# Two decoder blocks on one core: sliding attention by pairs of heads, on two row halves and two column halves

## What is computed

```
q = proj[..., :OFF_K].reshape(b, l, ATTN_HEADS, HEAD_DIM)          # 16 heads of 64
k = proj[..., OFF_K:OFF_V].reshape(b, l, ATTN_KV_HEADS, HEAD_DIM)  # 4 heads of keys
v = proj[..., OFF_V:OFF_Z].reshape(b, l, ATTN_KV_HEADS, HEAD_DIM)
attn = windowed_gqa_sink(q, k, v, attn_sink[i])
...
s = jnp.einsum('bnqgrd,bnkgd->bngrqk', qb, kw) * (d ** -0.5) + bias[None]
m = jnp.maximum(jnp.max(s, axis=-1, keepdims=True), sink_f)
p = jnp.exp(s - m)
denom = jnp.sum(p, axis=-1, keepdims=True) + jnp.exp(sink_f - m)
o = jnp.einsum('bngrqk,bnkgd->bnqgrd', (p / denom), vw)
...
merged = (jax.nn.sigmoid(gate_a) * (attn @ w_attn_branch[i])
          + jax.nn.sigmoid(gate_b) * (ssd @ w_ssd_branch[i]))
```

## Time and profile before

| | |
|---|---|
| median of 3 runs | 2693.75 us (2691.79 to 2695.16) |
| profiled execution, its own time | 2694.09 us |
| its span | 2692.3 us |
| PE, busy share | 96% |
| DVE, ACT busy share | 55%, 43% |
| share of the chain that ended last: PE, DVE, ACT | 79%, 13%, 5% |
| matmul instructions | 12498 |
| granted PE clock, mean | 0.984 |
| DMA, mean | 84 GB/s |

### The profile page before, as it was taken

One profiled execution on the slowest core, in us unless ns is written; L12 is line 12 of the kernel. 1 busy time (PEld: TensorE's weight loads), 2 busy tenths in 40 slices (PEclk: granted clock), 3 DMA queues, 4 the chain that ended last, 5 costly groups with the idle time before them and its releaser, 6 DMA issues.

```text
span 2692.3 us, 31915 instructions
## 1 busy us (share of the span) xinstructions
PE 2591.8 (96%) x12498; PEld 2110.0 (78%) x12498; DVE 1471.4 (55%) x2343; ACT 1155.8 (43%) x2068; POOL 146.3 (5%) x144
## 2 busy tenths in 40 slices
PE   7999999999999999999999999999999999999998
PEld 5888778888676778888787888888777887788886
DVE  5554454433556555334369887886555355453343
ACT  4254443322356644223255666655244344442232
POOL 1110000000100010000001000100000010000000
PEclk9999999999999999999989999999999999999999
DMA  4212123653222122232223112123211243223331
GB/s 138 71 56 67 61 77 102 135 132 102 79 92 77 63 79 94 94 102 95 81 56 102 56 55 77 57 71 87 73 33 40 71 141 110 71 94 99 100 99 63
DMA packets 201110, 225.47 MB, mean 84 GB/s; under 512 B 25152, under 2 KB 133984, under 8 KB 200704
## 3 DMA queue, kind: packets, MB, share of 16 engines
q1 hardware_dynamic: 200960, 223.43, 27.6%
HBM read 213.96 MB, written 9.44 MB: 83 GB/s over the span
## 4 chain that ended last, share of the span: by engine, by line
PE 79%; DVE 13%; ACT 5%; issue 2%; POOL 0%; DMA 0%; DVEq 0%; POOLq 0%; SPq 0%; ACTq 0%
PE bank L1767 21%; PE bank L1769 20%; PE bank L1768 20%; DVE CV L2458 3%; PE bank L1773 2%; DVE wlo L2234 2%; PE bank L1774 2%; PE bank L1775 2%; PE bank L1785 2%; PE bank L1970 1%; PE bank L1802 1%; PE bank L1951 1%; DVE E L2507 1%; ACT whi L2017 1%; PE bank L1866 1%
## 5 line engine op out<-in xcount | busy, mean ns | idle before, releaser
L2234 DVE TENSOR_TENSOR wlo<-raw,whi 128x1024 fp32r<-128x1024 f32 (+1 forms) x389 | 489.4, 1263 | 738.0 <-ACT whi L2017 735.8
L2017 ACT ACTIVATE whi<-raw 128x1024 fp32r<-128x1024 f32 (+1 forms) x389 | 408.5, 1057 | 652.8 <-PE bank L1769 611.6
L1767 PE MATMUL bank<-XAh,whi 128*128 128x512 f32 x1536 | 618.8, 403 | 19.8 <-DVE XAl L2242 10.9
L1768 PE MATMUL bank<-XAl,whi 128*128 128x512 f32 x1536 | 604.6, 394 | 0.0
L1769 PE MATMUL bank<-XAh,wlo 128*128 128x512 f32 x1536 | 604.3, 393 | 0.0
L1767 PEld LDWEIGHTS bank<-XAh,whi 128*128 128x128 f32 x1536 | 292.1, 190 | 97.6 <-issue 32.2
L1769 PEld LDWEIGHTS bank<-XAh,wlo 128*128 128x128 f32 x1536 | 291.9, 190 | 63.2
L1768 PEld LDWEIGHTS bank<-XAl,whi 128*128 128x128 f32 x1536 | 292.4, 190 | 59.1 <-issue 0.7
L1767 PE MATMUL bank<-XBh,whi 128*128 128x512 f32 x816 | 324.2, 397 | 3.0 <-DVE XBl L2240 1.7
L1769 PE MATMUL bank<-XBh,wlo 128*128 128x512 f32 x816 | 318.0, 390 | 0.0
L1768 PE MATMUL bank<-XBl,whi 128*128 128x512 f32 x816 | 317.8, 389 | 0.0
(11 more groups left out here) (326 smaller groups left out, 3449.0 us busy)
## 6 DMA issues: line engine op xcount, KB each, us to landing
raw<-in_w_in SPq DMA_DIRECT2D x68, 512.0 KB, 3.7
raw<-in_up SPq DMA_DIRECT2D x64, 512.0 KB, 3.5
raw<-in_down SPq DMA_DIRECT2D x64, 512.0 KB, 3.7
raw<-in_a_w_in SPq DMA_DIRECT2D x32, 512.0 KB, 4.0
raw<-in_w_up SPq DMA_DIRECT2D x32, 512.0 KB, 3.6
raw<-in_w_down SPq DMA_DIRECT2D x32, 512.0 KB, 3.6
raw<-in_w_kv SPq DMA_DIRECT2D x16, 512.0 KB, 3.5
raw<-in_w_ssd_branch SPq DMA_DIRECT2D x16, 512.0 KB, 3.4
```

The lines of the kernel that those rows point to most:

```text
L1767: pe.matmul(out, wh[:, w, c], xh[:, x, 0:s.ntok], start=st, stop=False)
L1768: pe.matmul(out, wh[:, w, c], xl[:, x, 0:s.ntok], start=False, stop=False)
L2017: act.activation(s.hi, s.raw, ACT.Copy).then_inc(s.whi[0], 1)
L2234: dve.tensor_tensor(s.lo, s.raw, s.hi.bitcast(F32), ALU.subtract).then_inc(s.wlo[0], 1)
```

## The change

Heads are issued by pairs. Both heads of a pair use the same key head, but lie in the two row halves of one Q tile, in the weights' own order. So the keys are needed in both halves: a second tile `KD` holds `KW` with its halves exchanged, written by two transfers on SP's queue (`swap_k`). A step of scores is now one query block of both heads, two matmuls on the two row halves, into two banks. A step of values does all ten products of both heads alternately, on the two column halves of one bank. `SW` and `AW` become one ring of six. `KD` takes 4 KB a partition, and `NRAW` goes from 4 to 3, which gives 4 KB back. The pipeline holds three pairs, in the order 0 to 7, and `scoring` lets a third pair start its scores only when one of two is past its norms.

```
-NRAW, NW = 4, 3
+NRAW, NW = 3, 3
...
+    KD = sb("KD", [P, 2, S], scope=both)
...
+    def keys_evac(j, i, b, m):
+        yield from keys_rows(j, i, b, m)
+        if j[1]:
+            qk["swapped"] = add("swap_k", dst=KD, src=KW, ready=qk["k", 1], land=sig("swapped", 32)).land
...
-        return two_tiles([(64 * x, 64) for i in (2 * n, 2 * n + 1) for x in heads_of[i]], rows_evac(Q_tile, "q", n, free), ring=ring, piece=piece, gate=lambda: free in w_free)
+        return two_tiles([(n * 256, 256)], rows_evac(Q_tile, "q", n, free), ring=ring, piece=piece, gate=lambda: free in w_free)
...
-        SW = Ring([Slot(sb(f"SW{i}", [P, 4, 384], scope=sc)) for i in range(3)])
-        AW = Ring([Slot(sb(f"AW{i}", [P, 4, 384], scope=sc)) for i in range(3)])
+        SW = Ring([Slot(sb(f"SW{i}", [P, 4, 384], scope=sc)) for i in range(6)])
...
+        def head_pair(hp):
+
+            kv = hp // 2
+            keys = [(KW, KD)[(kv + x) % 2] for x in range(2)]
...
+            while (started[p.pieces] and not p.hurry) or scoring["n"] == 1 or not SW.room(2) or not ring_all.room(3) or ("q", hp) not in qk:
                 yield WAIT
...
+            ss = [SW.take(), SW.take()]
+            for j in range(4):
...
+                s1 = add("wi_mm", Q=Q_tile(hp), kws=keys, kv=kv, j=j, banks=bs, q_ready=qk["q", hp], k_ready=qk["k", kv // 2], swapped=qk["swapped"], mm=[sig("wi.mm"), sig("wi.mm")])
+                s2 = add("wi_bias", ss=ss, j=j, banks=bs, slopes=slopes, mm=s1.mm, pads=sw_pads, biased=[sig("wi.bias"), sig("wi.bias")])
...
+                if j == 1:
+                    yield from p.spaced(1)
+            begun, exps, normed = p.pieces, [], []
+            for x in range(2):
+                exps.append(add("wi_exp", s=ss[x], c=stw[:, 2 * hp + x, :], hd=2 * hp + x, slope=slopes[x], biased=s2.biased[x], top=sig("wi.top"), exp=sig("wi.exp")).exp)
+                yield
+                yield from p.spaced(1)
+            for x in range(2):
+                normed.append(add("wi_norm", s=ss[x], c=stw[:, 2 * hp + x, :], exp=exps[x], normed=sig("wi.norm")).normed)
+                yield
+                yield from p.spaced(1)
+            scoring["n"] -= 1
...
-        p.run(products_w(), pipeline((head_w(2 * hp + hx) for hp in (0, 2, 1, 3, 4, 6, 5, 7) for hx in range(2)), 6), starts=[9, 0])
+        p.run(products_w(), pipeline((head_pair(hp) for hp in range(8)), 3), starts=[9, 0])
...
+            for x, b in enumerate(s.banks):
+                rs = slice(64 * x, 64 * x + 64)
+                pe.matmul(b.t[:, 0:w], s.Q[rs, s.j * P:(s.j + 1) * P], s.kws[x][rs, s.kv // 2, lo * P:lo * P + w], start=True, stop=True).then_inc(s.mm[x][0], 1)
...
+                    for x, aw in enumerate(s.aws):
+                        m = pe.matmul(s.bank.t[x * 64:x * 64 + 64, j * P:(j + 1) * P], s.V[:, ks, s.kv * 64:s.kv * 64 + 64], aw.t[:, ks, q0:q0 + P], start=ks == lo, stop=ks == hi)
...
+        elif k == "swap_k":
+            on.wait_ge(*s.ready)
+            for x in range(2):
+                sp.dma_start(s.dst[64 * x:64 * x + 64, :, :], s.src[64 - 64 * x:128 - 64 * x, :, :]).then_inc(s.land[0], 16)
```

More of the change, by code:

```diff
@@ L1497, in branch_gemm @@
             return gemm(XB, 8, "w_attn_branch_2", [(hf * 512, 512)], fm4(), evac, ring=ring_all, piece=1)
[L1499 to L1504, removed]
+        def head_pair(hp):
+            kv = hp // 2
+            keys = [(KW, KD)[(kv + x) % 2] for x in range(2)]
+            slopes = [float(np.float32(2.0 ** (-8.0 * (2 * hp + x + 1) / 16))) for x in range(2)]
+            while (started[p.pieces] and not p.hurry) or scoring["n"] == 1 or not SW.room(2) or not ring_all.room(3) or ("q", hp) not in qk:
                 yield WAIT
             started[p.pieces] += 1
-            s = SW.take()
-            for j0 in (0, 2):
+            scoring["n"] += 1
+            ss = [SW.take(), SW.take()]
+            for j in range(4):
                 while not ring_all.room(2):
@@ L1516, in head_w @@
                 yield
-            begun = p.pieces
-            s3 = add("wi_exp", s=s, c=stw[:, hd, :], hd=hd, slope=slope, biased=s2.biased[1], top=sig("wi.top"), exp=sig("wi.exp"))
-            yield
[L1520 to L1546, removed]
@@ new lines, in head_pair @@
+            for x in range(2):
[3 more added lines that the diff above has]
+            scoring["n"] -= 1
+            aws, done = [], []
+            for x in range(2):
+                while not SW.room(1):
+                    yield WAIT
+                aws.append(SW.take())
+                for k0 in (0, 2):
+                    while not ring_all.room(2):
+                        yield WAIT
+                    bs = [ring_all.take(), ring_all.take()]
+                    s5 = add("wi_tr", s=ss[x], k0=k0, banks=bs, normed=normed[x], tr=[sig("wi.tr"), sig("wi.tr")])
+                    s6 = add("wi_aw", aw=aws[x], k0=k0, banks=bs, tr=s5.tr, scope_free=end, aw_done=[sig("wi.aw"), sig("wi.aw")])
+                    for b, v in zip(bs, s6.aw_done):
+                        b.free(v)
+                    yield
+                ss[x].free(s5.tr[1])
+                done.append(s6.aw_done[1])
+                yield from p.spaced(1)
@@ L1552, in head_w @@
+            yield from p.spaced(1)
+            while not ring_all.room(1) or ("v", 1) not in qk:
+                yield WAIT
+            ob = ring_all.take()
+            s7 = add("wi_val", V=VW, kv=kv, aws=aws, aw_ready=done, bank=ob, v_ready=[qk["v", x] for x in range(2)], val=sig("wi.val"))
+            for aw in aws:
+                aw.free(s7.val)
+            yield
+            yield from split_apart(XB, hp, ob.t[:, :], s7.val)
+            ob.free(XB.ready[hp])
             yield
         XB.open()
-        p.run(products_w(), pipeline((head_w(2 * hp + hx) for hp in (0, 2, 1, 3, 4, 6, 5, 7) for hx in range(2)), 6), starts=[9, 0])
+        p.run(products_w(), pipeline((head_pair(hp) for hp in range(8)), 3), starts=[9, 0])
@@ L2536, in dve_program @@
             on.wait_ge(*s.pads)
[L2537 to L2542, removed]
+            lo, w, off = win_span(s.j)
+            for x, (t, b) in enumerate(zip(s.ss, s.banks)):
+                on.room(t)
+                on.wait_ge(*s.mm[x])
+                dve.scalar_tensor_tensor(out=t.t[:, s.j, off:off + w], in0=b.t[:, 0:w], scalar=0.125 / s.slopes[x], in1=K.Rt[:, off:off + w], op0=ALU.mult, op1=ALU.add).then_inc(s.biased[x][0], 1)
         elif k == "wi_exp":
```

25 lines of the change are left out of this document (9 added, 16 removed).

## The result

The changed kernel takes **2654.43 us** (median of 4 runs, 2652.97 to 2657.42), the kernel before 2693.88 (2691.79 to 2695.16): a ratio of 0.9856 with a 95% interval of 0.9839 to 0.9873. The forecast was 2655.0, with 2644 to 2672 as its range. The profiled execution is the shortest of the four, 2652.97 us with a span of 2651.2, so it lies 1.5 us under the median; the spans of the two profiles differ by 41.1 us, the medians by 39.5.

A forecast was written before the change was run, and what follows sets the result against it. TensorE, busy 96% of the span, was taken to bound the kernel. From 2694.1 us, streams save 32.0, waits and clock 8.5, and the raw slot costs 1: 2654.6, said as 2655, own range 2645 to 2664, wider range 2644 to 2672.

The forecast's parts named there:

- scores: Score blocks of the attention stage: two heads on two row halves cost as one, 14.1 us saved.
- transposes: Transposes in the stage: as many as before but cut into more blocks, 2.4 us more.
- values: Value blocks in the stage: two heads on two column halves take 2.33 us a pair, 18.7 us saved.
- waits in the stage: TensorE's waits between first score and last value product: 8.7 us before, 6 us after.
- lost to the clock: Slow stretches in the stage: 9.2 us lost before, 3.4 us after, from two stretches of 3.4 us.
- raw slot: Weight loads, four slots to three: costs only at the full queue near 556 us; 1 us taken.
- The rivals that keep a packing from working: In the stage: only scores run side by side, 2672 us, chance 0.08; or nothing does, 2689 us, chance 0.04.
- Packing in part: Scores and values: the second half costs a quarter of its own passes, 8.6 us more, 2663 us; chance 0.06.
- The chain to the norm: Last score block to first transpose: 15.9 us in the second gate branch against 13.8 of cover, about 2 us wait.
- Both rivals with a wait in every period: Norm chain waits in all seven periods: 2 us each, 2671 us, chance 0.10; or 5.0 each, 2709 us, chance 0.04.
- Switches: Products beside value blocks: eight blocks fewer spare eight exits and entries at 0.2 us, 1.6 us saved.
- The rival that nothing runs side by side: Scores and values in the stage: no packing works, 2689 us; chance 0.04.

The follow-up runs named there:

- early_norm3: Changed kernel with a pair's two exponentials issued back to back and the first norm right behind them, ahead of the half unit of products: 2648.3 us.
- ali4: Changed kernel with four raw slots again, keys still swapped early, room from five scratch tiles and tensors laid into idle ones: 2648.63 us.
- both_apart: Changed kernel with both heads' scores on one row half and a pair's values issued one head after the other: 2676.2 us.
- best4: Changed kernel with four raw slots, early key swap, and a pair's exponentials back to back with the first norm right behind: 2643.69 us.
- raw3: Kernel before the change with three raw slots in place of four, nothing else: 2698.09 us beside 2693.46.
- val_apart: Changed kernel with a pair's values issued one head after the other instead of alternately: 2662.41 us.
- late1s5: Changed kernel with four raw slots, keys swapped only when the stage begins, and five scratch tiles in place of six: 2652.56 us.
- score_onehalf: Changed kernel with both heads' scores on the lower row half, the second head using the first one's rows: 2670.97 us.

## Why the prediction was right

The account by its terms, for the 1250 matmuls of the stage and what lies ahead of them. The first four rows are sums of steps from start to start. A block with a wait or a slow stretch in it is counted at the mean of its like without one (one block of products has no such like; there its wait is taken off).

| term | predicted, us | measured, us |
|---|---|---|
| scores | 37.6 to 23.5: -14.1 | 37.6 to 23.3: -14.3 |
| transposes | +2.4 | 18.7 to 20.8: +2.1 |
| values | 37.3 to 18.6: -18.7 | 37.2 to 18.7: -18.6 |
| products, with exits and entries spared | -1.6 | 152.1 to 150.7: -1.4 |
| waits in the stage | 8.7 to 6: -2.7 | 9.5 to 5.3: -4.2 |
| lost to the clock | 9.2 to 3.4: -5.8 | 9.2 to 1.7: -7.5 |
| in no row above | | -0.4 |
| raw slot, as the later first score | +1 | +2.7 |
| behind the 1250 matmuls | | +0.1 |
| sum | -39.5 | -41.5 (profiles, to the last matmul), -39.5 (medians) |

- **Both packings** are shown, not only fitted: each edit that takes one away brings its passes back at 0.107 us apiece: a score block grows by 0.43 or 0.64 us, four and six times that, 17.0 in all, the value blocks by 14.4 in all, less than the 17.1 of their passes by the seam. The rivals that keep a packing from working fall. Packing in part falls too: a V block would have been 2.33 + 2.14 / 4 = 2.87 us by the prediction's quarter, and is 2.33. The Trainium skill ("TensorE: Matmul & The Clock Gate", Part 3) has factors of 3.07 for four row tiles and 2.38 for three column tiles, 0.77 and 0.79 of the ideal. They do not carry over to two halves here. The passes alone show the full factor of two; whole blocks, entry and exit included, go from 1.06 to 0.63 and from 1.49 to 0.85 us, 0.84 and 0.88 of the ideal, and a value block from the 4.47 worked out for blocks apart to 2.33, 0.96 of it.
- **The chain to the norm** is where the prediction put it and as long. In the wait at 2075.5 its order is the predicted one (gate product, second maximum, weight rest, gate product, norm), and from the last score block to the norm's end it takes 15.8 us (2059.7 to 2075.4; predicted 15.9). In the wait at 2051.1 the last score block ends at 2035.9. The first head's exponentials end at 2041.4 (5.5 us; predicted 5.6), the second head's at 2048.3 (12.4; 11.4), the norm at 2051.1 (15.2; 15.9). Here the weight rest stands where the prediction had the first gate product, and only one gate product comes ahead of the norm; VectorE waits 3.5 us for whi before the rest. PE had work for 13.8 us, as worked out, and waited 1.4. The wait at 1938.9 has no gate product in its chain, but the weight rest, as predicted. That this chain causes all three waits is shown by early_norm3. Both rivals with a wait in every period fall: there are three.
- **Waits before.** The prediction counted 8.7 us. The list of the stage has two lines more, 0.5 and 0.2 us, which it left out; the waits of the kernel before are 9.5 us in all.
- **The clock.** One slow stretch came in the stage and not two. Of the change's three waits, only the longest was followed by one (2076.0). This term was a guess by precedent and came out 1.7 us too dear. The precedent itself was read too kindly: the two waits of 1.9 us before have slow stretches of 6.8 and 3.4 behind them, not of 3.4 each. Nothing in the prediction says why only one came, so this part of the gain is luck.
- **The raw slot** is the term that was mis-sized: 1 us taken, 2.7 in the later first score, inside the bounds (0 to 5.7, and 3.4 of clock). The 2.7 are 4.46 near 557 us, less 0.82 by which this profile was ahead before, and less 0.90 that it won back further on, with no slot in it; over all profiles a slot costs 4.1. The failed step is "PE had no wait thanks to the units split ahead ... I take 1", and with it a sign named in advance: PE was to have no wait there, and has one of 2.7. The mechanism is the one named: ACT waits 25.0 us for loads between 500 and 600 us, six times (before 10.1, twice), PE 2.7, and a slow stretch of 3.4 follows. With four slots PE's wait and the slow stretch are away (ali4). I had read ACT's 9.12 us as spare because PE had no wait, and had not worked out how much of the cover was left behind them; the middle of the bounds would have been nearer.
- **Switches.** The products beside the blocks take 1.4 us less, for 1.6 worked out. No run tests this term alone.
- So the four terms of the stream were right to 0.2 us together (-32.2 for -32.0), and the sum was close partly because two errors met: waits and clock gained 3.6 us more than worked out (12.1 for 8.5), and the raw slot cost 1.7 more in this profile (about 3 over all).
- **Order against packing.** With waits and slow stretches absent in both, both_apart needs 244.7 us for the 1250 matmuls and best4 213.6: the packing is worth 31.1 us of stream. The order alone takes the stage from 264.8 to 244.7, 20.1 us. That is hardly a shorter stream: by the table's first four rows the stream before is 245.6 us long, so 19.2 of the 20.1 are the waits and slow stretches that are gone. The change gives 6.9 of their sum back to waits and the clock: 20.1 + 31.1 - 6.9 = 44.3. The rival that nothing runs side by side was priced at 2689, and that case measures 2676.2; most of its error is the 9.4 us of waits and clock that I charged it, and 2.8 in the values' seams.
- **The rest** at nothing held: no wait for the swap, none for a memset of the pads.

## What to carry to other kernels

In this kernel two matmuls that use half the array's rows or columns each were had for the price of one when they stood next to each other in the stream, and rows of another place in the same kernel price the block, fixed part included. A stream that gets faster loses the cover of the chains beside it: price the waits for each case anew, since what the packed stream waits for, the unpacked one hides; here the packing saved 31.1 us of stream and 21.8 of time. A buffer given up in one stage is paid for wherever the queue is fullest; look there for how much of the cover is already used, and look for room in tensors that are idle while the new one lives.

## What the runs showed of the hardware

- **A seam overlaps by itself.** When 20 passes on one column half are followed by 20 on the other, three passes of each ran side by side: 4.13 us, and not 4.47.
- **A small shift moves slow stretches elsewhere.** raw3 lags the kernel before by 1.6 us behind 560, and its trace has a slow stretch at 756 that the other has not, while between 1370 and 1396 its granted clock is 0.61 and not 0.74. By the first score its lag is 3.2 us.
- **The length of a short wait did not decide whether a slow stretch followed.** In the change and in ali4 waits of PE of 1.8 and 1.4 us passed without one, and one of 2.0 had one. But in val_apart the wait of 1.8 us at 1938.5 is followed by one of 3.4 us, in late1s5 one of two waits of 2.0 us is (1942.0) and the other is not (2056.3), and in score_onehalf a wait of 1.7 us is followed by one of 6.8. So a wait of 1.4 to 2.0 us cost between itself and itself plus 3.4 us. What decides it, these runs do not show.
